# Token mixer of a two-layer trunk: projections reordered, stick queries and keys made with stationary weights, small attention steps regrouped, masks moved to VectorE

## The chip, the cores and the metric

The kernel runs on one core of a Trainium2 chip. The metric is the device time of one execution in microseconds (us). The engines are named as the profile names them: PE is TensorE (PEld its weight loads), DVE is VectorE, ACT is ScalarE, POOL is GpSimd, and SP issues most DMAs.

## The reference, cut to what matters

```python
h = x
for i in range(DEPTH):                                  # DEPTH 2, SEQ 256, D_MODEL 1024
    f = swiglu(rms_norm(h, ffn1_pre_g[i]), ffn1_w_gu[i], ffn1_w_down[i])     # D_FF 2816
    h = h + 0.5 * rms_norm(f, ffn1_post_g[i])
    u = rms_norm(h, mix_pre_g[i])
    sb_q, sb_k, sb_v, df_q, df_k, df_v, g_sb, g_df = jnp.split(u @ w_in[i], split_at, axis=-1)
    ...
    # stick breaking, 8 heads of 64:  z = q k^T / 8, strict causal mask
    log_one_minus = jnp.where(strict, jax.nn.log_sigmoid(-z), 0.0)
    later = lax.cumsum(log_one_minus, axis=3, reverse=True) - log_one_minus
    w = jnp.where(strict, jnp.exp(jax.nn.log_sigmoid(z) + later), 0.0)       # o_sb = w @ v
    ...
    # differential, 4 heads, two components of 64 each, rotary on df_q and df_k
    z = jnp.where(causal, z, -jnp.inf)
    probs = jax.nn.softmax(z, axis=-1)
    a = probs[:, :, 0] - lam * probs[:, :, 1]                                # o_df = rms_norm(a @ v)
    ...
    merged = jax.nn.sigmoid(g_sb) * y_sb + jax.nn.sigmoid(g_df) * y_df       # y = o @ w_branch
    h = h + rms_norm(merged @ w_out[i], mix_post_g[i])
    # then a second feed-forward part like the first, and a gated per-layer embedding
```

`w_in` has ten blocks of 512 columns: stick q, k, v, differential q, k, v, and four blocks of gates.

## The kernel before

All products are made in "exact" arithmetic: a float32 operand is split into a high part (fp32r) and a low part, and a product is hi\*hi + hi\*lo + lo\*hi. Weights come in units of 128x2048 float32, which are 512 rows by 512 columns of a `w_in` block. SP loads a unit into one of three slots; ACT makes its high part `w_hi` (`high`, L646, scaled by the norm's gain); DVE makes its low part `w_lo` (`low`, L1084, four instructions of 128x512); PE then uses it. A slot comes free when PE is through with the unit that stood in it.

The order of all work is written by hand, as one stream for each engine, with semaphores between them. The mixer of a layer is a loop over `m`. For m = 0 to 19 PE multiplies the two units of block j = m // 2 (half = m % 2) into two PSUM banks, one for each half `t` of the 256 tokens; m = 20 and 21 are the stick branch's output product. In iteration m ACT and DVE prepare unit m + 2, and do their part of the attention steps that stand at that place. On PE small steps stand either between the two token halves of unit m (`middle`) or behind it (`behind`).

A wide unit (`wide`, L1473 to L1475) has the activations stationary and 512 weight columns moving: 24 matmuls of 512 columns, result tokens x columns. The feed-forward loop also has a flat unit (`flat_gate_up`, L1591 and L1601): 128x128 blocks of the weights are stationary and the tokens move, 16 matmuls of 512 columns (high and low tokens side by side) and 16 of 256, result columns x tokens.

The stick and differential q and k come out as tokens x columns; ACT copies each to `slab` with the row scale (`keep`), POOL applies the rotary to the two differential ones (`rope`, four instructions for each of the two token halves), and PE transposes each (`turn_four`, 8 transposes, L1692) into `sbq_t`, `sbk_t`, `dfq_t`, `dfk_t`. `v_sb` and `v_df` are scaled into place by DVE (L1314).

The four stick pairs go through `stick_scores` (PE), three ACT and four DVE steps (`stick_soft`), `stick_later` (PE), exponential (ACT), `cap` (DVE), `stick_values` (PE). The four differential heads go through `masked` and `diff_scores` (PE), maximum (DVE), exponential (ACT), mixing (DVE), `diff_turn` (PE), copy (ACT), `diff_values` (PE) and a norm (ACT, POOL, DVE). The tables at L54 to L59 say at which half iteration each stands: stick pair n has its scores at m = 6 + 3n, differential head n at m = 12 + 2n. `kept(i, j, t)` makes PE wait until half t of block j has left PSUM. In the profile and in the rows below, `ps` is the PSUM.

## Time and profile before

| | |
|---|---|
| median of 3 runs | 1187.6 us (1187.34 to 1187.7) |
| the profiled execution | 1187.24 us, of it 1185.2 us from the first to the last instruction |
| busy | PE 1173.8 us (99%), DVE 848.7 us (72%), ACT 719.9 us (61%), POOL 92.9 us (8%) |
| TensorE's granted clock | 0.999 of full speed |
| mixer, layer 0 | m = 3 to 19 run from 218.66 us to 337.06 us |

In the timeline a matmul's busy time reaches past the start of the next one, since they are pipelined; what a matmul costs in a stream is the distance between two starts. The same holds, by a few hundredths of a microsecond, for DVE and ACT.

### The profile page before, as it was taken

The page shows a single profiled execution, that of the slowest core. Times are in us where ns is not written, and L with a number is a line of the kernel's source. Part 1 is how long each engine was busy: PE and PEld are TensorE (multiplying, and loading weights), DVE is VectorE, ACT ScalarE, POOL GpSimd, SP SyncE. Part 2 cuts the span into 40 slices and gives each one's busy share as a digit, 9 for nine tenths or more (in the row PEclk, how much of TensorE's full clock was granted, in tenths as well). Part 3 has the DMA queues.
Part 4 walks back from the last instruction along what each step waited for, and adds up shares of the span by engine and source line. Part 5 has one row for each costly group of instructions (what it writes and reads, how often), then busy time and mean ns, then how long its engine had stood idle before and what let it go on. Part 6 is the DMA issues. An engine that isn't in the chain of part 4 may idle for free.

```text
span 1185.2 us, 17137 instructions
## 1 busy us (share of the span) xinstructions
PE 1173.8 (99%) x6013; PEld 984.4 (83%) x6013; DVE 848.7 (72%) x1235; ACT 719.9 (61%) x1163; POOL 92.9 (8%) x157
## 2 busy tenths in 40 slices
PE   8999999999999999999999999999999999999997
PEld 7888888888788888888888888888877888888886
DVE  5766777588667866676787776676976776767666
ACT  6655556666665755564685655576656666555555
POOL 4000000042000100000110000010600010000002
PEclk9999999999999999999999999999999999999999
DMA  8656565553345555556546565756343456556550
GB/s 269 232 183 201 171 218 192 198 178 118 132 178 178 178 196 194 191 172 230 178 158 203 175 209 178 249 162 208 114 159 133 169 178 213 175 179 206 183 196 36
DMA packets 138654, 215.36 MB, mean 182 GB/s; under 512 B 6958, under 2 KB 97904, under 8 KB 138608
## 3 DMA queue, kind: packets, MB, share of 16 engines
q1 hardware_dynamic: 135808, 208.43, 52.9%
q10 hardware_dynamic: 2576, 6.29, 1.6%
q8 instruction: 28, 0.46, 0.2%
q14 instruction: 18, 0.15, 0.0%
q0 software_dynamic: 224, 0.04, 0.0%
HBM read 213.68 MB, written 1.05 MB: 181 GB/s over the span
## 4 chain that ended last, share of the span: by engine, by line
PE 96%; ACT 2%; DVE 1%; DMA 1%; issue 0%; POOL 0%; SPq 0%; DVEq 0%; POOLq 0%; ACTq 0%
PE ps L1591 22%; PE ps L1473 19%; PE ps L1475 19%; PE ps L1474 19%; PE ps L1601 12%; PE ps L1520 2%; PE ps L1692 1%; DMA raw<-in_w_ple_proj 1%; PE ps L1723 1%; DVE w_lo L1084 0%; ACT w_hi L646 0%; PE ps L1736 0%; PE ps L1709 0%; ACT prob L804 0%; PE ps L1752 0%
## 5 line engine op out<-in xcount | busy, mean ns | idle before, releaser
L1084 DVE SCALAR_TENSOR_TENSOR w_lo<-raw,g_layer,w_hi 128x512 fp32r<-128x512 f32 (+1 forms) x504 | 369.6, 793 | 131.4 <-ACT w_hi L646 131.4
L646 ACT ACTIVATE w_hi<-raw,g_layer 128x512 fp32r<-128x512 f32 (+1 forms) x524 | 346.9, 732 | 113.5 <-PE ps L1601 97.0
L1591 PE MATMUL ps<-x_both,w_hi 128*128 128x512 f32 x1152 | 287.7, 392 | 0.0
L1473 PE MATMUL ps<-w_hi,x_both 128*128 128x512 f32 x640 | 257.4, 402 | 0.0
L1475 PE MATMUL ps<-w_hi,x_both 128*128 128x512 f32 x640 | 250.2, 391 | 0.0
L1474 PE MATMUL ps<-w_lo,x_both 128*128 128x512 f32 x640 | 249.6, 390 | 0.0
L1591 PEld LDWEIGHTS ps<-x_both,w_hi 128*128 128x128 f32 x1152 | 209.4, 189 | 39.3 <-issue 0.3
L1081 DVE TENSOR_TENSOR w_lo<-raw,w_hi 128x1024 fp32r<-128x1024 f32 x114 | 134.7, 1221 | 55.0 <-ACT w_hi L643 55.0
L643 ACT ACTIVATE w_hi<-raw 128x1024 fp32r<-128x1024 f32 x114 | 114.7, 1052 | 91.7 <-PE ps L1475 91.6
L1601 PEld LDWEIGHTS ps<-x_both,w_lo 128*128 128x128 f32 x1152 | 152.6, 191 | 8.4
L1601 PE MATMUL ps<-x_both,w_lo 128*128 128x256 f32 x1152 | 156.0, 283 | 0.0
L1473 PEld LDWEIGHTS ps<-w_hi,x_both 128*128 128x128 f32 x640 | 120.2, 188 | 27.1 <-issue 3.3
L1475 PEld LDWEIGHTS ps<-w_hi,x_both 128*128 128x128 f32 x640 | 120.1, 188 | 26.1
L1474 PEld LDWEIGHTS ps<-w_lo,x_both 128*128 128x128 f32 x640 | 120.4, 188 | 22.8
L1473 PE MATMUL ps<-w_hi,ht_hi 128*128 128x512 f32 x320 | 124.9, 390 | 0.0
L1475 PE MATMUL ps<-w_hi,ht_lo 128*128 128x512 f32 x320 | 124.6, 389 | 0.0
L1474 PE MATMUL ps<-w_lo,ht_hi 128*128 128x512 f32 x320 | 124.5, 389 | 0.0
L728 ACT ACTIVATE glu<-glu 128x512 f32<-128x512 f32 x36 | 22.8, 633 | 78.5 <-DVE glu L1130 78.5
L1475 PEld LDWEIGHTS ps<-w_hi,ht_lo 128*128 128x128 f32 x320 | 60.1, 188 | 12.5
L1474 PEld LDWEIGHTS ps<-w_lo,ht_hi 128*128 128x128 f32 x320 | 60.1, 188 | 12.4
L1473 PEld LDWEIGHTS ps<-w_hi,ht_hi 128*128 128x128 f32 x320 | 60.1, 188 | 12.3
L536 POOL TENSOR_TENSOR ms_post<-mean_post,eps_half 128x1 f32<-128x1 f32 x8 | 2.4, 305 | 548.6 <-ACT tmp L694 548.6
(217 smaller groups left out, 1008.7 us busy)
## 6 DMA issues: line engine op xcount, KB each, us to landing
raw<-in_ffn_w_gu SPq DMA_DIRECT2D x170, 512.0 KB, 4.6
...
```

Of the source, the lines that this page charges most:

```text
L643: last = act.activation(w_hi[:, s, part], raw[:, s, part], ACT.Copy)
L646: last = act.activation(w_hi[:, s, part], raw[:, s, part], ACT.Copy, scale=g_layer[:, g:g + 1])
L728: act.activation(glu_g, glu_g, ACT.Silu).then_inc(silu_done, 2)
L1081: last = dve.tensor_tensor(w_lo[:, s, part], raw[:, s, part], whi[:, part], ALU.subtract)
L1084: last = dve.scalar_tensor_tensor(out=w_lo[:, s, part], in0=raw[:, s, part], scalar=g_layer[:, g:g + 1], in1=whi[:, part], op0=ALU.mult, o ...
L1473: pe.matmul(dst, x_h, w_h, start=first, stop=False, **group)
L1474: pe.matmul(dst, x_h, w_l, start=False, stop=False, **group)
L1475: return pe.matmul(dst, x_l, w_h, start=False, stop=last, **group)
L1520: mm = pe.transpose(x_bank(i, q, idx)[:, k * P:(k + 1) * P], src[:, (4 * n + k) * P:(4 * n + k + 1) * P], ident[:, :])
L1591: mm = pe.matmul(dst, w_hi[:, s, cols], x_both[:, :, 4 * half + k, :], start=half == 0 and k == 0, stop=stop and k == 3, skip_group_check= ...
L1601: mm = pe.matmul(bank(FLAT_BANK[j])[:, 0:SEQ], w_lo[:, s, cols], x_hi[:, 4 * half + k, :], start=False, stop=False, skip_group_check=True)
L1692: mm = pe.transpose(dst[:, k * SEQ + t * P:k * SEQ + (t + 1) * P], src[:, t, k * P:(k + 1) * P], ident[:, :])
```

## The change

- Blocks of `w_in` are taken in another order: differential q, differential k, stick q, stick k, differential v, stick v, gates (`W_IN_BLOCK`). Block j still has m = 2j and 2j + 1.
- Stick q and k (m = 4 to 7) are made as flat units (`flat_win`). Their results stand as columns x tokens, so their two `turn_four` go. Instead ACT copies the part made of low tokens to `flat_copy` (`keep_flat`), and DVE adds the other part and multiplies by the row scale (`add_flat`, four instructions for a block). The row scale is needed along the free axis, so it is spread by DVE (`spread_r`), transposed by PE (`turn_r`, two transposes) and copied by ACT (`keep_r`) at m = 1 and 2.
- POOL's rotary for differential q stands behind block 0 instead of block 3, that of k behind block 1 instead of block 4. The transposes stand behind m = 4 and 6 instead of 9 and 11.
- Stick pair n and differential head n share their places: scores of both behind m = 7 + 3n; `stick_later` and `diff_turn` in the middle of m = 9 + 3n, `diff_values` behind it. `stick_values` stand in the middle of 12, behind 13 and 16, and in the middle of 19, and write to a bank of their own (3 or 5).
- The causal mask of the differential scores was two bf16 matmuls of 256 columns (`masked`); now it is two minimum instructions on DVE in PSUM (`cap_df`), 128x256 each, for each head.

```diff
-SBQ, SBK, SBV, DFQ, DFK, DFV = range(6)
+DFQ, DFK, SBQ, SBK, DFV, SBV = range(6)
+W_IN_BLOCK = (3, 4, 0, 1, 5, 2, 6, 7, 8, 9)
 
 PAIRS = SB_HEADS // 2
-SB_SCORE = {12 + 6 * n: n for n in range(PAIRS)}
-SB_LATER = {15 + 6 * n: n for n in range(PAIRS)}
-SB_VALUE = {17 + 6 * n: n for n in range(PAIRS)}
-DF_Z0, DF_T0, DF_P0 = 12, 13, 14
-BY_ACT = (0, 1, 3, 4, 6, 7, 8, 9)
-QK_ORDER = {SBQ: 0, SBK: 1, DFQ: 2, DFK: 3}
+SB_SCORE = {15 + 6 * n: n for n in range(PAIRS)}
+SB_LATER = {18 + 6 * n: n for n in range(PAIRS)}
+SB_VALUE = {slot_: n for n, slot_ in enumerate((24, 27, 33, 38))}
+DF_SCORE = {7 + 3 * n: n for n in range(DF_HEADS)}
+DF_TURN = {9 + 3 * n: n for n in range(DF_HEADS)}
+BY_ACT = (DFQ, DFK, 6, 7, 8, 9)
...
+        df_slabs = [[x[:, t, 0:W] for t in range(TT)] for x in (tmp, gates[:, 0, :, :])]
+        flat_copy = w_att[:, :, 0:SEQ]
...
+        SB_FLAT = {SBQ: (0, 4), SBK: (0, 2)}
+        VALUE_BANK = (3, 3, 3, 5)
+
+        def outs(n):
+            return bank(VALUE_BANK[n])[:, 0:SEQ].rearrange("p (t q) -> p t q", t=TT)
...
+            def keep_flat(i, m, j):
+
+                for x, b in enumerate(SB_FLAT[j]):
+                    n = 4 * i + 2 * (j - SBQ) + x
+                    wait_product(act, win_done, 10 * i + j + 1, i, U_WIN + m, x)
+                    act.wait_ge(flat_added, n)
+                    act.activation(flat_copy, flat_pair(b)[1], ACT.Copy, scale=SB_D ** -0.5 if j == SBQ else 1.0
+                                   ).then_inc(flat_kept, 1)
 
...
+            def add_flat(i, j):
+
+                for x, b in enumerate(SB_FLAT[j]):
+                    n = 4 * i + 2 * (j - SBQ) + x + 1
+                    dst = (sbq_t, sbk_t)[j - SBQ][:, 2 * x:2 * x + 2, :]
+                    dve.wait_ge(flat_kept, n)
+                    dve.scalar_tensor_tensor(out=dst, in0=flat_pair(b)[0], scalar=SB_D ** -0.5 if j == SBQ else 1.0,
+                                             in1=flat_copy, op0=ALU.mult, op1=ALU.add).then_inc(flat_added, 1)
+                    dve.wait_ge(flat_added, n)
+                    dve.wait_ge(r_kept, nth_r(i, 1))
+                    dve.tensor_tensor(dst, dst, r_cols.to_broadcast([P, 2, SEQ]), ALU.mult).then_inc(sb_ready, 1)
+
...
                     if m == 1:
+                        dve.wait_ge(pre_scale, 8 * i + 4)
+                        spread_r(i)
...
-                    if m in (5, 11):
+                    if m in (5, 7):
+                        add_flat(i, m // 2)
+                    if m in (9, 11):
                         j = m // 2
                         for t in range(TT):
                             wait_product(dve, win_done, 10 * i + j + 1, i, U_WIN + m, t)
                             dve.tensor_scalar((v_sb, v_df)[j == DFV][:, t, :], bank(WIN_BANK[j % 2][t]),
...
+                        for c in range(2):
+                            last = dve.tensor_tensor(diagonal(DF_BANK[c]), diagonal(DF_BANK[c]),
+                                                     cap_df[:, :, :].to_broadcast([P, 2, P]), ALU.min)
+                        last.then_inc(d_capped, 1)
+                        dve.wait_ge(d_capped, DF_HEADS * i + hd + 1)
...
-                pe.wait_ge(sb_turned, 2 * i + 2)
+                pe.wait_ge(sb_ready, 4 * i + 3 + n // 2)
                 if n:
-                    pe.wait_ge(os_split, PAIRS * i + n)
+                    pe.wait_ge(s_weight, PAIRS * i + n)
...
-                pe.wait_ge(kept_dve, 4 * i + 2)
+                kept(i, (SBV, SBV, 7, 8)[n], 1)
+                if n:
+                    pe.wait_ge(os_split, PAIRS * i + n)
...
-                for c in range(2):
-                    masked(DF_BANK[c], mask_df)
                 for c, rows in enumerate(HEAD_ROWS):
-                    pe.matmul(bank(DF_BANK[c])[:, 0:P], dfq_t[rows, hd, 0:P], dfk_t[rows, hd, 0:P], start=False,
+                    pe.matmul(bank(DF_BANK[c])[:, 0:P], dfq_t[rows, hd, 0:P], dfk_t[rows, hd, 0:P], start=True,
                               stop=False, skip_group_check=True)
                 for c, rows in enumerate(HEAD_ROWS):
...
                 pe.wait_ge(d_kept, DF_HEADS * i + hd + 1)
-                pe.wait_ge(kept_dve, 4 * i + 4)
+                kept(i, DFV, 0)
                 dst, c = bank(DF_BANK[1]), slice(hd * DF_V, (hd + 1) * DF_V)
                 pe.matmul(dst[:, 0:P], mixed_t[:, 0:P], v_df[:, 0, c], start=True, stop=True, skip_group_check=True)
                 pe.matmul(dst[:, P:SEQ], mixed_t[:, P:SEQ], v_df[:, 0, c], start=True, stop=False,
                           skip_group_check=True)
+                kept(i, DFV, 1)
...
                 stick(i, 2 * m)
-                if 0 <= m - DF_P0 < 2 * DF_HEADS and (m - DF_P0) % 2 == 0:
-                    diff_values(i, (m - DF_P0) // 2)
+                if m in DF_TURN:
+                    diff_turn(i, DF_TURN[m])
...
-                    turn_four(pair(QK_PAIR), slab).then_inc(qk_turned, 1)
+                    turn_r(i, 1, QK_PAIR)
                 if m == 4:
-                    pe.wait_ge(kept_act, 16 * i + 4)
-                    pe.wait_ge(sb_turned, 2 * i + 1)
-                    turn_four(pair(QK_PAIR), slab).then_inc(qk_turned, 1)
-                if m == 9:
+                    pe.wait_ge(r_kept, nth_r(i, 1))
                     pe.wait_ge(roped, 4 * i + 2)
-                    pe.wait_ge(sb_turned, 2 * i + 2)
-                    turn_four(pair(QK_PAIR), slab).then_inc(qk_turned, 1)
-                if m == 11:
+                    turn_four(pair(QK_PAIR), df_slabs[0]).then_inc(qk_turned, 1)
+                if m == 6:
                     pe.wait_ge(roped, 4 * i + 4)
                     pe.wait_ge(df_turned, 2 * i + 1)
-                    turn_four(pair(QK_PAIR), slab).then_inc(qk_turned, 1)
+                    turn_four(pair(QK_PAIR), df_slabs[1]).then_inc(qk_turned, 1)
                 stick(i, 2 * m + 1)
-                if 0 <= m - DF_Z0 < 2 * DF_HEADS and (m - DF_Z0) % 2 == 0:
-                    diff_scores(i, (m - DF_Z0) // 2)
-                if 0 <= m - DF_T0 < 2 * DF_HEADS and (m - DF_T0) % 2 == 0:
-                    diff_turn(i, (m - DF_T0) // 2)
+                if m in DF_SCORE:
+                    diff_scores(i, DF_SCORE[m])
+                if m in DF_TURN:
+                    diff_values(i, DF_TURN[m])
...
+            def bank_free(i, j, t):
+
+                if j in (DFV, SBV):
+                    pe.wait_ge(flat_added, 4 * i + 2 * (j - DFV) + 2)
+                elif j > SBV:
+                    kept(i, j - 2, t)
+                    if t == 1 and j in (7, 9):
+                        pe.wait_ge(os_split, PAIRS * i + {7: 2, 9: 3}[j])
...
+            def flat_win(i, m, j, half, x):
+
+                s, b = slot(U_WIN + m), SB_FLAT[j][x]
+                if half == 0:
+                    if x:
+                        kept(i, j - 2, 1)
+                    elif j == SBK:
+                        pe.wait_ge(flat_added, 4 * i + 1)
+
+                def long(stop):
+
+                    for n in range(2):
+                        dst = bank(b + n).rearrange("p (a n) -> p a n", a=2)
+                        for k in range(4):
+                            cols = slice(k * W + (2 * x + n) * P, k * W + (2 * x + n + 1) * P)
+                            mm = pe.matmul(dst, w_hi[:, s, cols], x_both[:, :, 4 * half + k, :],
+                                           start=half == 0 and k == 0, stop=stop and k == 3, skip_group_check=True)
+                    return mm
...
+                    return mm
+
...
+                short()
+                mm = long(True)
+                if x == 0:
+                    mm.then_inc(win_done, 1)
+                return mm
 
             def mixer(i):
                 def first_win(s, t, before):
...
+                        if j in SB_FLAT:
+                            mm = flat_win(i, m, j, half, t)
+                            if t == 0:
+                                middle(i, m)
+                            continue
+                        if half == 0:
+                            bank_free(i, j, t)
...
```

DVE around the iterations 4 to 6: behind the small `neg_lam` steps stood the low part of unit 7 and the scaling of `v_sb`.

```order
L1304 TENSOR_TENSOR neg_lam<-lam_e 128x1 [waits lam_exp]
L1307 TENSOR_TENSOR neg_lam<-neg_lam,neg_init 128x1 [waits lam_step]
L1084 SCALAR_TENSOR_TENSOR w_lo<-raw,g_layer,w_hi 128x512 [waits hi_ready]
L1084 SCALAR_TENSOR_TENSOR w_lo<-raw,g_layer,w_hi 128x512
L1084 SCALAR_TENSOR_TENSOR w_lo<-raw,g_layer,w_hi 128x512 [waits hi_ready]
L1084 SCALAR_TENSOR_TENSOR w_lo<-raw,g_layer,w_hi 128x512
L1314 TENSOR_SCALAR v_sb<-ps,r_pre 128x512 [waits win_done]
L1314 TENSOR_SCALAR v_sb<-ps,r_pre 128x512 [waits units_used]
```

Now the copy of `dfq_t` stands ahead of that low part (L1100), and `add_flat` for stick q behind it.

```order
L1338 TENSOR_TENSOR neg_lam<-lam_e 128x1 [waits lam_exp]
L1341 TENSOR_TENSOR neg_lam<-neg_lam,neg_init 128x1 [waits lam_step]
L1369 COPY dfq_t<-ps 128x1024 [waits qk_turned]
L1100 SCALAR_TENSOR_TENSOR w_lo<-raw,g_layer,w_hi 128x512 [waits hi_ready]
L1100 SCALAR_TENSOR_TENSOR w_lo<-raw,g_layer,w_hi 128x512
L1100 SCALAR_TENSOR_TENSOR w_lo<-raw,g_layer,w_hi 128x512 [waits hi_ready]
L1100 SCALAR_TENSOR_TENSOR w_lo<-raw,g_layer,w_hi 128x512
L1301 SCALAR_TENSOR_TENSOR sbq_t<-ps,w_att 128x512 [waits flat_kept]
L1305 TENSOR_TENSOR sbq_t<-sbq_t,prob 128x512 [waits r_kept,flat_added]
L1301 SCALAR_TENSOR_TENSOR sbq_t<-ps,w_att 128x512 [waits flat_kept]
```

The first of these `add_flat` instructions is behind one more long copy and the whole low part; PE's m = 6 waits for it (`flat_added`).

PE where scores begin: a differential head's scores stood by themselves behind m = 12, ahead of the next unit.

```order
L1698 MATMUL ps<-mask_df,ident_b 128x2x128 [waits df_turned]
L1698 MATMUL ps<-mask_df,ident_b 128x2x128
L1749 MATMUL ps<-dfk_t,dfq_t 128x128 x2
L1752 MATMUL ps<-dfk_t,dfq_t 128x256 x2
L1473 MATMUL ps<-w_hi,x_both 128x512 [waits split_done]
L1474 MATMUL ps<-w_lo,x_both 128x512
```

Now the first stick pair and the first head stand together behind m = 7, whose last flat matmuls are the first row here.

```order
L1877 MATMUL ps<-x_both,w_hi 128x512 x8
L1746 MATMUL ps<-sbq_t,sbk_t 128x256 [waits sb_ready]
L1746 MATMUL ps<-sbq_t,sbk_t 128x256
L1749 MATMUL ps<-sbq_t,sbk_t 128x128 x2
L1786 MATMUL ps<-dfk_t,dfq_t 128x128 [waits df_turned]
L1786 MATMUL ps<-dfk_t,dfq_t 128x128
L1789 MATMUL ps<-dfk_t,dfq_t 128x256 x2
L1512 MATMUL ps<-w_hi,x_both 128x512 [waits flat_added,split_done]
```

The two masks are gone, and the scores of both kinds stand without a unit between them; m = 8 begins in the last row.

PE at the first stick values: before, they stood behind m = 8, three units after `v_sb`'s own (m = 5).

```order
L1474 MATMUL ps<-w_lo,x_both 128x512
L1475 MATMUL ps<-w_hi,x_both 128x512
L1736 MATMUL ps<-w_att,v_sb 64x128 [waits kept_dve,s_capped]
L1736 MATMUL ps<-w_att,v_sb 64x128 x5
L1473 MATMUL ps<-w_hi,x_both 128x512 [waits split_done]
L1474 MATMUL ps<-w_lo,x_both 128x512
```

Now they stand in the middle of m = 12, half a unit after `v_sb`'s own (m = 11), with `stick_later` (the last two rows here) and then `diff_turn` behind them.

```order
L1513 MATMUL ps<-w_lo,x_both 128x512
L1514 MATMUL ps<-w_hi,x_both 128x512
L1775 MATMUL ps<-w_att,v_sb 64x128 [waits kept_dve,s_capped]
L1775 MATMUL ps<-w_att,v_sb 64x128 x5
L1760 MATMUL ps<-sp_hi,neg_tri 128x384 [waits s_soft]
L1761 MATMUL ps<-sp_hi,neg_one 128x128
```

The wait for `kept_dve` is for both halves of `v_sb`. In the same way the first `diff_values` now stand right behind m = 9, the unit that makes `v_df`.

## Rows read from the trace of the kernel before

**Rows 1.** The page: busy us of each engine, TensorE's clock, the chain by engine
```profile
PE 1173.8 (99%) x6013; PEld 984.4 (83%) x6013; DVE 848.7 (72%) x1235; ACT 719.9 (61%) x1163; POOL 92.9 (8%) x157
...
PEclk9999999999999999999999999999999999999999
...
PE 96%; ACT 2%; DVE 1%; DMA 1%; issue 0%; POOL 0%; SPq 0%; DVEq 0%; POOLq 0%; ACTq 0%
```

**Rows 2.** The chain in order of time (start us, us, what), feed-forward loop
```profile
45.33 1.81 PE ps L1591 x8
...
61.92 1.81 PE ps L1591 x8
```

**Rows 3.** Timeline of PE in the mixer, layer 0 (start us, us, engine, line, op, out<-in, count [idle])
```profile
218.66 1.03 PE L1692 MATMUL ps<-ident,tmp 128*128 128x128 f32 x8
219.45 0.48 PE L1473 MATMUL ps<-w_hi,x_both 128*128 128x512 f32 x1
219.77 0.40 PE L1474 MATMUL ps<-w_lo,x_both 128*128 128x512 f32 x1
...
230.24 0.39 PE L1475 MATMUL ps<-w_hi,x_both 128*128 128x512 f32 x1
```

**Rows 4.** Timeline of PE: stick scores, stick values, differential scores, each standing alone
```profile
239.29 0.39 PE L1475 MATMUL ps<-w_hi,x_both 128*128 128x512 f32 x1
...
240.80 0.40 PE L1474 MATMUL ps<-w_lo,x_both 128*128 128x512 f32 x1
...
255.17 0.39 PE L1475 MATMUL ps<-w_hi,x_both 128*128 128x512 f32 x1
...
256.63 0.39 PE L1474 MATMUL ps<-w_lo,x_both 128*128 128x512 f32 x1
...
284.39 0.39 PE L1698 MATMUL ps<-mask_df,ident_b 128*128 128x256 bf16 x2
284.71 0.49 PE L1749 MATMUL ps<-dfk_t,dfq_t 64*128 64x128 f32 x4
...
285.90 0.39 PE L1474 MATMUL ps<-w_lo,x_both 128*128 128x512 f32 x1
```

**Rows 5.** Timeline of PE: longest idle in the mixer, longest of all after the start
```profile
310.40 0.39 PE L1475 MATMUL ps<-w_hi,x_both 128*128 128x512 f32 x1
311.01 0.49 PE L1767 MATMUL ps<-v_df,mixed_t 128*128 128x128 f32 x2 [0.21 <-ACT mixed_t L813]
...
9.63 0.50 PE L1473 MATMUL ps<-w_hi,p_hi 128*128 128x512 f32 x1 [1.02 <-DVE w_lo L1062]
```

**Rows 6.** Timeline of DVE: low parts before, during and after the rotary
```profile
212.93 2.74 DVE L1084 SCALAR_TENSOR_TENSOR w_lo<-raw,g_layer,w_hi 128x512 fp32r<-128x512 f32 x4 [2.94 <-ACT w_hi L646]
...
246.44 4.78 DVE L1084 SCALAR_TENSOR_TENSOR w_lo<-raw,g_layer,w_hi 128x512 fp32r<-128x512 f32 x4
...
267.08 1.21 DVE L1329 COPY dfq_t<-ps 128x1024 f32<-128x1024 f32 x1
268.21 5.32 DVE L1084 SCALAR_TENSOR_TENSOR w_lo<-raw,g_layer,w_hi 128x512 fp32r<-128x512 f32 x4
```

**Rows 7.** Timeline of POOL (rotary) and of ACT (the first kept product)
```profile
247.09 1.30 POOL L577 TENSOR_TENSOR tmp<-tmp,rope_c 128x512 f32<-128x512 f32 x1 [35.67 <-ACT tmp L842]
...
252.51 1.30 POOL L577 TENSOR_TENSOR tmp<-tmp,rope_c 128x512 f32<-128x512 f32 x1
...
214.03 1.24 ACT L842 ACTIVATE tmp<-ps,r_query 128x512 f32<-128x512 f32 x2
```

**Rows 8.** Timeline of DVE: one differential and one stick step, value projection
```profile
285.68 1.02 DVE L1323 TENSOR_REDUCE neg_max<-ps 128x2 f32<-128x256 f32 x2 [1.76 <-PE ps L1752]
...
287.60 0.76 DVE L1255 TENSOR_TENSOR soft<-soft,cap_sb 128x256 f32<-128x256 f32 x2
...
290.98 0.75 DVE L1084 SCALAR_TENSOR_TENSOR w_lo<-raw,g_layer,w_hi 128x512 fp32r<-128x512 f32 x1
...
278.42 1.39 DVE L1314 TENSOR_SCALAR v_df<-ps,r_pre 128x512 f32<-128x512 f32 x2
```

More of the change, by code:

```diff
@@ L242, in trunk_kernel @@
         d_score = sem("d_score")
+        d_capped = sem("d_capped")
         d_max = sem("d_max")
@@ new lines, in diff_keep, with diff_square @@
+            def diff_keep(i, hd):
+                act.wait_ge(d_turned, DF_HEADS * i + hd + 1)
+                act.activation(mixed_t[:, :], bank(DF_BANK[0])[:, 0:384], ACT.Copy).then_inc(d_kept, 1)
+            def diff_square(i, hd):
+                act.wait_ge(d_value, DF_HEADS * i + hd + 1)
+                if hd:
+                    act.wait_ge(d_square, DF_HEADS * i + hd)
+                for t in range(TT):
+                    last = act.activation(squares[:, t * P:(t + 1) * P], bank(DF_BANK[1])[:, t * P:(t + 1) * P],
+                                          ACT.Square, scale=DF_V ** -0.5, accum_out=mean_sub[:, t:t + 1])
+                last.then_inc(d_square, 1)
@@ L1285, in mixer @@
                     elif 2 * m in SB_VALUE:
-                        low(i, U_WIN + m + 2, 8 + 4 * (m % 2), halves=(0,))
+                        gain = 8 + 4 * (m % 2) if m < 18 else None
+                        low(i, U_WIN + m + 2, gain, halves=(0,))
                         stick_out(i, 2 * m)
-                        low(i, U_WIN + m + 2, 8 + 4 * (m % 2), halves=(1,))
+                        low(i, U_WIN + m + 2, gain, halves=(1,))
                     elif m < 18:
@@ L1735, in stick_values @@
                         c = (2 * n + e) * SB_D
-                        mm = pe.matmul(bank(SB_BANK[t])[rows, OUT_COLS], v_sb[:, keys, c:c + SB_D],
+                        mm = pe.matmul(outs(n)[rows, t, :], v_sb[:, keys, c:c + SB_D],
                                        w_att[:, e, cols], start=first, stop=last, skip_group_check=True)
@@ new lines, in flat_win, with short @@
+            def flat_win(i, m, j, half, x):
[13 more added lines that the diff above has]
+                    return mm
+                def short():
+                    for n in range(2):
+                        for k in range(4):
+                            cols = slice(k * W + (2 * x + n) * P, k * W + (2 * x + n + 1) * P)
+                            mm = pe.matmul(bank(b + n)[:, 0:SEQ], w_lo[:, s, cols], x_hi[:, 4 * half + k, :],
+                                           start=False, stop=False, skip_group_check=True)
+                    return mm
+                if half == 0:
+                    long(False)
+                    return short()
+                short()
[3 more added lines that the diff above has]
+                return mm
```

181 lines of the change are left out of this document (81 added, 100 removed).

## Prediction, made before the changed kernel was run

> **What bounds the kernel now.** I read the page first: PE is busy 1173.8 of 1185.2 us, 96% of the chain that ended last is PE, and its clock stays at full speed (2.4 GHz) in all 40 slices [rows 1]. So the time is the sum of PE's starts plus its few waits. I then took PE's timeline for prices, as distances between starts, since busy times overlap; and DVE's, POOL's and ACT's timelines to see what else could come to stand in PE's way.
>
> In the mixer the two wide units from 219.45 to the start at 230.24 and 0.23 more take 11.02 us for 48 matmuls, 0.09 of it a slow start [rows 3]: 5.46 us a unit, 0.2275 a matmul. One turn of the feed-forward loop is 16.59 us [rows 2]; less a 24-matmul unit of 5.46 that leaves 5.57 for each of its two flat units. Between the starts at 310.40 and 311.01, 0.61 instead of 0.23, PE waited longest inside the mixer [rows 5]. Everything else there is PE's own work, so a change must take work from PE, and must not make it wait.
>
> **PE's work, for one layer.** (1) The `turn_four` of stick q and k go. One costs 219.77 - 218.66 - 0.23 = 0.88 us, eight transposes at 0.11 [rows 3]: -1.76. `turn_r` comes, two transposes: +0.22.
>
> (2) Stick scores alone cost 240.80 - 239.29 less two matmuls = 1.05. Differential scores alone cost 285.90 - 284.39 - 0.23 = 1.28, of which the masks 0.32 [rows 4]. A group of 64-row matmuls pays on entering and leaving: the matmul ahead of the stick scores and the one behind take some 0.1 more each, and so do the first and last inside. Joined and without masks I count 1.05 + 1.28 - 0.32 - 0.3 = 1.71 (between 1.5 and 2.0, if two or no such payments go). Four times -0.62 is -2.5.
>
> (3) Stick values alone cost 256.63 - 255.17 - 0.455 = 1.0 [rows 4]. Two of the four now stand ahead of scores and share their entry: -0.3 each, -0.6 (0 if a 64-column and a 64-row group share nothing). Later and turn steps are joined four times instead of twice: -0.1. Fewer restarts: -0.2.
>
> (4) Four wide units become flat: 4 x (5.57 - 5.46) = +0.45.
>
> (5) The wait of 0.4 goes with the place it stood at.
>
> Sum: -1.76 + 0.22 - 2.5 - 0.6 - 0.1 - 0.2 + 0.45 - 0.4 = -4.9 a layer, -9.8 us for two (bounds -7.5 and -11). The minimum instructions on DVE replace PE work; DMAs stay, only the block's address changes; POOL loses its bf16 set-up, in the first microseconds, where nobody waits for it.
>
> **New waits, for one layer.** All three come from DVE, which works in strict order and now has more ahead of what PE wants.
>
> *A, at m = 6.* This flat unit writes banks 0 and 1, which the first half of stick q (m = 5) filled; they are free once `add_flat` has read them. PE: m = 2 ends at 218.66 as now; 0.22, 5.46, 5.57, 0.88 and 5.57 take it to 236.4.
>
> DVE: its low part from 212.93 takes 2.74 us for four instructions, 0.665 each [rows 6]. POOL's rotary now follows the product ACT keeps at 214.03 (first half 0.68 later, then 0.14 to POOL) [rows 7], so at 214.85. One token half took 5.4 us (247.09 to 252.51) [rows 7], and there are four. So POOL works until 236.5, where before this stretch was free of it. Under it DVE's four take 4.78 us, the first of them ahead of POOL's start at 247.09, so (4.78 - 0.67) / 3 = 1.37 each; and 5.32, 1.33 each [rows 6, 7]. I take 1.37. From 212.93: three at the free pace, one slow, then the row spread and the lambda sums (an estimate, 1.0) to 217.4; the low parts of units 4, 5 and 6, 12 x 1.37 = 16.4, to 233.8; lambda again and the copy of `dfq_t`, 1.21 under POOL's work [rows 6] and 0.3, to 235.3; unit 7's low part, nearly one instruction slow and three free, 3.3, to 238.6; `add_flat`, as one low instruction with its end 0.75, to 239.3; 0.1 for PE to start. PE waits from 236.4 to 239.4: 3.0 us. At 1.25 each it is 2.2, at 1.5 it is 4.0. If the rotary did not slow DVE at all it is 0: 13 instructions fewer at 1.37, 9 us, are more than the 3.0.
>
> Why DVE is slowed: the Trainium skill, SBUF - State Buffer, section "SBUF: two separate sides", says that GpSimd and a VectorE instruction with two SBUF inputs take one port pair in turn, each for its whole instruction. By that rule 16 POOL instructions let 16 such DVE instructions through in 21.6 us, 1.35 each, which makes A 2.9 us where my rows make it 3.0. It speaks against moving the rotary to where DVE is needed within half a unit.
>
> *B, behind m = 9.* `diff_values` need `v_df`, m = 9's own product. The joint scores behind m = 7 end (call it 0). DVE is held by `add_flat` of stick k for 0.8; then two minima 0.78 (as two `cap` on SBUF, 0.76 [rows 8]; not seen on PSUM, 0.7 to 1.1), the diff and stick step 5.30 (285.68 to 290.98) [rows 8], two low parts 5.3, `cap` 0.73, `v_df` first half 0.7: 13.7. PE: 0.1 + 5.46 + 2.73 + 1.43 (later and turn) + 2.73 = 12.45. It waits 1.4, and some 0.2 more for the second half: 1.6 (1.0 to 2.2).
>
> *C, in the middle of m = 12.* `stick_values` need both halves of `v_sb`, m = 11's product. From the end of the scores behind m = 10: DVE 0.1 + 0.78 + 5.30 + 2.65 (low part) + 1.39 (`v_sb`, as the two of `v_df` [rows 8]) = 10.2, and 0.1 to start PE: 10.3. PE is there after 0.1 + 5.46 + 2.73 = 8.3. Wait 2.0 (1.7 to 2.5). For the later pairs values and gates are kept early, and I find no wait: `diff_turn` has 1.0 us or more to spare each time.
>
> Waits: 3.0 + 1.6 + 2.0 = 6.6 a layer. Each starts from a point where DVE waited for PE, so they add up.
>
> **Sum.** 2 x (6.6 - 4.9) = +3.4 on the profiled 1187.24, so 1190.6; that execution is 0.36 below the median, which gives 1191.0.
>
> **Rivals.** *Free rotary.* A is small, because POOL's instructions run faster when DVE yields, or DVE gets in more often than in rows 6. For it: rows 6 are two samples, taken while DVE did other things in between. Against: both are at 1.33 or more. With A at 0.5: 2 x (4.1 - 4.9) = -1.6, 1186.0. The total turns from slower to faster once A is under 1.3 us.
>
> *All hidden.* None of the waits is there, because DVE has more room than I count: -9.8, 1177.8. Against it: B and C are sums of rows seen in this very order of work, and only 1 to 2 us of error is in each.
>
> *DVE stays behind.* A wait at m = 6 also delays stick k's `add_flat`, so the first scores behind m = 7 wait as well (I count DVE ready 0.1 us before PE), and later turns miss their 1.0 us: 1 to 2 us more a layer, 1191.5 to 1196.
>
> *The clock falls.* PE's longest pause now between matmuls after the start is 1.02 us, with full clock behind it [rows 5, 1]; A would be three times that, and what the clock then does no row shows. If it fell to 1.2 GHz for some 3 us behind each A, it would cost 1.5 us each: +3, 1194. The Trainium skill, TensorE: Matmul & The Clock Gate, section "Why this matters for your kernels", advises against idle gaps of about this length in the middle of a kernel; by it this rival would be live.
>
> *The regrouping saves less on PE* (no shared entries, bf16 masks cheaper than 0.32): -7.5 instead of -9.8, 1193.
>
> **How the numbers follow.** Forecast with three waits, 1188.5 to 1193.5: 0.48. DVE stays behind or the clock falls: 0.14. Less saved on PE: 0.05. Free rotary, 1184.5 to 1188: 0.22. All hidden: 0.11. The range 1184.0 to 1194.5 leaves out all hidden and the far end of the slow rivals. A measurement of this kernel can tell 0.2% (2.4 us) from no change. Above 1190.0: two thirds of the forecast's share and all but little of the slow ones, 0.51; within: 0.26, from the forecast's lower part and half of free rotary; below 1185.2: 0.23. The likeliest case's own range is 1188.5 to 1193.5.
>
> **What the profile after would show.** PE idle of about 3 us ahead of the first matmul of the third flat unit, released by DVE's `sbq_t`; about 1.5 ahead of the first `diff_values`, by `v_df`; about 2 ahead of the first `stick_values`, by `v_sb`; none of these three and the rest is wrong with them. Low parts of 1.2 to 1.8 us each on DVE between 215 and 236 us. The joint scores 1.7 us from start to start, 0.88 for each of two `turn_four` less, flat units at 5.57. The clock at full speed throughout, or this is where the forecast errs. It is wrong above all if DVE keeps pace with the rotary, or if PE's small groups cost other than the sum of their rows.

## The result, and the profile after

The changed kernel takes 1201.7 us (median; 1201.3 to 1202.4) against 1187.5 us before (1187.3 to 1187.7): ratio 1.0121, 95% interval 1.0107 to 1.0135. It is slower by 14.2 us. The profiled execution spans 1199.6 us, where that of before spanned 1185.2. Of all executions of the kernels below, four took 1452 to 6678 us; the ratios leave these slow runs out, the medians hold them and move by at most 0.3 us for it.

The page of the changed kernel: busy us of each engine, PE's busy share and TensorE's clock in 40 slices, and the chain that ended last by engine.
```profile
PE 1172.9 (98%) x6033; PEld 989.5 (82%) x6033; DVE 867.2 (72%) x1269; ACT 717.2 (60%) x1161; POOL 92.9 (8%) x154
...
PE   8999999899999999999999999998999999999997
...
PEclk9999999999999999999999999999999999999999
...
PE 89%; DVE 8%; ACT 1%; issue 1%; DMA 1%; SPq 0%; DVEq 0%; POOLq 0%; POOL 0%; ACTq 0%
```
Against [rows 1], DVE's share of the chain went from 1% to 8%. That names the engine to look at, not the size of the loss: 7% of the span would be 84 us. The rest of the page shows little: two of PE's slices read 8 instead of 9, PE's busy time is nearly unchanged (1172.9 against 1173.8 us), because matmuls that run slowly count as busy, and a clock that falls for a few us did not change the digit of any 30 us slice. So I went on to what PE waits for (us in total, times, longest), and to PE's timeline.
```profile
PE ps L1877 <- DVE sbq_t L1301: 9.4, 2, 4.7
PE ps L1775 <- DVE v_sb L1350: 4.4, 2, 2.2
PE ps L1804 <- DVE v_df L1350: 1.7, 2, 0.9
```
```profile
234.72 2.00 PE L1877 MATMUL ps<-x_both,w_hi 128*128 128x512 f32 x8
241.43 3.75 PE L1877 MATMUL ps<-x_both,w_hi 128*128 128x512 f32 x8 [4.71 <-DVE sbq_t L1301]
244.98 0.41 PE L1886 MATMUL ps<-x_both,w_lo 128*128 128x256 f32 x1
...
255.56 0.70 PE L1746 MATMUL ps<-sbq_t,sbk_t 64*128 64x256 f32 x4
...
257.07 0.50 PE L1512 MATMUL ps<-w_hi,x_both 128*128 128x512 f32 x1
...
269.33 0.39 PE L1514 MATMUL ps<-w_hi,x_both 128*128 128x512 f32 x1
270.59 0.46 PE L1804 MATMUL ps<-v_df,mixed_t 128*128 128x128 f32 x2 [0.87 <-DVE v_df L1350]
...
286.63 0.39 PE L1514 MATMUL ps<-w_hi,x_both 128*128 128x512 f32 x1
289.19 0.88 PE L1775 MATMUL ps<-w_att,v_sb 128*64 128x128 f32 x12 [2.18 <-DVE v_sb L1350]
290.00 0.69 PE L1760 MATMUL ps<-sp_hi,neg_tri 128*128 128x384 f32 x1
290.49 0.31 PE L1761 MATMUL ps<-sp_hi,neg_one 128*128 128x128 f32 x1
```
The three forecast waits are there, at the forecast places, in both layers. As a distance between starts less one matmul, the first is 4.87 us in layer 0 and 4.89 in layer 1 (A); the others are 1.03 (B, and 0.2 for the second half of `v_df`) and 2.34 (C). Two rows show something else. The eight flat matmuls from 241.43 take 3.75 us, where the eight from 234.72 took 2.00. The 128x384 matmul at 290.00 holds the engine for 0.49 us until the next start; the same four at m = 9 take 0.17 to 0.23 (265.37 to 266.40), and run 9 below shows 0.28 at this very place. The same trace by stretches (us, busy us of PE, PEld, DVE, ACT and POOL with instructions, granted clock, DMA share, GB/s) says why:
```profile
230.00:236.00 6.00, 6.00 (x41) 5.45 (x40) 6.00 (x5) 3.16 (x5) 5.78 (x5) 1.00 0.54 175
236.00:241.00 5.00, 0.72 (x4) 0.26 (x2) 4.97 (x8) 0.00 (x0) 0.69 (x1) 0.78 0.66 210
241.00:243.00 2.00, 1.57 (x4) 1.31 (x5) 1.93 (x4) 1.62 (x3) 0.00 (x0) 0.50 0.52 96
243.00:246.00 3.00, 3.00 (x13) 2.52 (x12) 3.00 (x5) 1.42 (x3) 0.00 (x0) 0.57 0.77 290
246.00:250.00 4.00, 4.00 (x30) 3.67 (x29) 0.07 (x1) 0.74 (x2) 0.00 (x0) 1.00 0.69 215
286.00:289.00 3.00, 1.01 (x5) 0.51 (x3) 3.00 (x6) 1.40 (x3) 0.00 (x0) 1.00 0.13 14
289.00:291.00 2.00, 1.80 (x15) 1.66 (x16) 1.85 (x5) 0.38 (x1) 0.00 (x0) 0.74 0.80 266
291.00:294.00 3.00, 3.00 (x13) 2.79 (x13) 2.00 (x4) 1.19 (x2) 0.00 (x0) 0.60 0.59 180
```
The granted clock, full before the wait, is 0.50 behind A and at 0.6 to 0.7 on average behind C: it fell to 1.2 GHz and came back. I size that by distances between starts: from A's end to the `turn_four` of k 7.57 us, where kernels with a full clock there show 5.69; from the first stick values to the next `diff_values` 6.67 us against 5.10. So the clock costs 1.9 us behind A (1.4 in layer 1) and 1.6 behind each C.

DVE's timeline shows why A is 4.9 and not 3.0:
```profile
213.10 3.78 DVE L1100 SCALAR_TENSOR_TENSOR w_lo<-raw,g_layer,w_hi 128x512 fp32r<-128x512 f32 x4 [2.98 <-ACT w_hi L656]
216.81 0.83 DVE L1136 COPY mixed_t<-r_pre 128x256 f32<-128x256 f32 x1
217.56 0.82 DVE L1332 TENSOR_TENSOR lam_pr<-lam_layer 128x128 f32<-128x128 f32 x1
...
218.62 16.92 DVE L1100 SCALAR_TENSOR_TENSOR w_lo<-raw,g_layer,w_hi 128x512 fp32r<-128x512 f32 x12
235.46 1.25 DVE L1338 TENSOR_TENSOR neg_lam<-lam_e 128x1 f32<-128x1 f32 x1
...
236.81 1.22 DVE L1369 COPY dfq_t<-ps 128x1024 f32<-128x1024 f32 x1
237.95 2.73 DVE L1100 SCALAR_TENSOR_TENSOR w_lo<-raw,g_layer,w_hi 128x512 fp32r<-128x512 f32 x4
240.60 0.68 DVE L1301 SCALAR_TENSOR_TENSOR sbq_t<-ps,w_att 128x512 f32<-128x512 f32 x1
```
The twelve large instructions take (235.46 - 218.62) / 12 = 1.40 us each, forecast 1.37. What I had not priced is the small ones under the rotary: a copy of 128x256 takes 0.83 us, a product of 128x128 0.82, and a difference of 128x1 1.25. In the run without the rotary they take 0.41, 0.28 and 0.15.

### The profile page after: what moved, and what is told of

It is laid out like the page before. It is cut to its first block, busy times and chain, and to the rows that moved or that the text cites. A ratio compares the mean times of both kernels' runs of the same rounds, so it can differ in the third digit from the quotient of the medians.

```text
span 1199.6 us, 17214 instructions
## 1 busy us (share of the span) xinstructions
PE 1172.9 (98%) x6033; PEld 989.5 (82%) x6033; DVE 867.2 (72%) x1269; ACT 717.2 (60%) x1161; POOL 92.9 (8%) x154
## 4 chain that ended last, share of the span: by engine, by line
PE 89%; DVE 8%; ACT 1%; issue 1%; DMA 1%; SPq 0%; DVEq 0%; POOLq 0%; POOL 0%; ACTq 0%
PE ps L1633 22%; PE ps L1512 16%; PE ps L1514 16%; PE ps L1513 16%; PE ps L1643 11%; DVE w_lo L1100 5%; PE ps L1559 2%; PE ps L1877 2%; PE ps L1886 1%; DMA raw<-in_w_ple_proj 1%; PE ps L1760 1%; PE ps L1775 1%; PE ps L1746 0%; DVE soft L1257 0%; PE ps L1734 0%
## 5 line engine op out<-in xcount | busy, mean ns | idle before, releaser
L1100 DVE SCALAR_TENSOR_TENSOR w_lo<-raw,g_layer,w_hi 128x512 fp32r<-128x512 f32 (+1 forms) x504 | 375.7, 807 | 134.5 <-ACT w_hi L656 134.5
L1512 PE MATMUL ps<-w_hi,x_both 128*128 128x512 f32 x576 | 231.2, 401 | 0.0
L1514 PE MATMUL ps<-w_hi,x_both 128*128 128x512 f32 x576 | 225.1, 391 | 0.0
L1513 PE MATMUL ps<-w_lo,x_both 128*128 128x512 f32 x576 | 224.7, 390 | 0.0
L1512 PEld LDWEIGHTS ps<-w_hi,x_both 128*128 128x128 f32 x576 | 108.4, 188 | 23.7 <-issue 3.0
L1514 PEld LDWEIGHTS ps<-w_hi,x_both 128*128 128x128 f32 x576 | 108.1, 188 | 23.5
L1513 PEld LDWEIGHTS ps<-w_lo,x_both 128*128 128x128 f32 x576 | 108.5, 188 | 20.7
```

The lines of the kernel that those rows point to most:

```text
L1100: last = dve.scalar_tensor_tensor(out=w_lo[:, s, part], in0=raw[:, s, part], scalar=g_layer[:, g:g + 1], in1=whi[:, part], op0=ALU.mult, o ...
L1512: pe.matmul(dst, x_h, w_h, start=first, stop=False, **group)
L1513: pe.matmul(dst, x_h, w_l, start=False, stop=False, **group)
L1514: return pe.matmul(dst, x_l, w_h, start=False, stop=last, **group)
```

## Experiments

All twelve change only a few lines. Times are medians; the kernel before gave 1187.3 to 1187.5 beside them. The account behind them adds up, for each run, what its own trace shows: waits and slow stretches read as above, against the changed kernel's.

**1. No rotary.** POOL rotates one head of eight only (the output is changed by that).
```diff
-                    pool.tensor_tensor(slab_c[:, t, :] ..., x, rope_c ..., ALU.mult)
-                    pool.tensor_tensor(y[:, :, 0:32], ..., ALU.mult)
-                    pool.tensor_tensor(y[:, :, 32:64], ..., ALU.mult).then_inc(rope_parts, 1)
+                    pool.tensor_tensor(slab_c[:, t, 0:64], xs[:, 0:64], rope_c[:, t, :], ALU.mult).then_inc(rope_parts, 1)
                     pool.wait_ge(rope_parts, 4 * i + 2 * k + t + 1)
-                    pool.tensor_tensor(xs, slab_c[:, t, :], rope_b[:, t, :], ALU.add).then_inc(roped, 1)
+                    pool.tensor_tensor(xs[:, 0:64], slab_c[:, t, 0:64], rope_s[:, t, :], ALU.add).then_inc(roped, 1)
```


> The changed kernel with POOL's rotary cut to one head of eight: per token half two instructions of 128x64 instead of four on 128x512 (the output is changed by that). Theory (POOL's rotary holds DVE back until stick k's first half must wait for add_flat, and the clock then falls): the wait of 4.9 us inside m = 6 and the half-rate matmuls behind it (2.0 us) are gone in both layers, the waits behind m = 9 and in the middle of m = 12 stay: 1201.7 - 13.8 = 1188. Rival (DVE is late by its own order of work, POOL counts for little): a wait of 2 us or more stays at m = 6, 1195 or more.

Measured 1186.5, ratio 0.9988 (0.9978 to 0.9998). What PE waits for now begins with these lines; the one at m = 6 is gone:
```profile
PE ps L1767 <- DVE v_sb L1342: 4.4, 2, 2.2
PE ps L1796 <- DVE v_df L1342: 1.7, 2, 0.9
```
Without the rotary DVE even waits for ACT ahead of two low parts in that stretch. With DVE's order as it is, A needs the rotary; B and C stand without it. It is 1.5 us better than expected, and in the profiled execution the clock did not fall behind C in layer 1, which is 1.6.

**2. v_df and v_sb by ACT.**
```diff
+                    elif j in (SBV, DFV):     # ACT's keep
+                        act.activation((v_sb, v_df)[j == DFV][:, t, :], src, ACT.Copy,
+                                       scale=r_pre[:, t:t + 1]).then_inc(kept_dve, 1)
-                    if m in (9, 11):          # DVE
-                        ... dve.tensor_scalar((v_sb, v_df)[j == DFV][:, t, :], ...)
```


> The changed kernel with v_df and v_sb (units 9 and 11) scaled and kept by ACT instead of DVE. Theory (DVE's own order makes the waits B and C; the clock falls behind C): the 2.3 us in the middle of m = 12, the 2.0 us of half-rate matmuls behind it and nearly all of the 1.25 us behind m = 9 go: 1201.7 - 11 = 1191. The wait at m = 6 stays 4.9. Rival (something else that DVE does at m = 11 is as late, as stick's cap): C shrinks by the two v_sb instructions alone, 1.4 us a layer, and the clock still falls: 1198.

Measured 1193.3, ratio 1.0053 (1.0036 to 1.0070). C is gone with the half-rate stretch behind it, and of B 0.6 remains:
```profile
PE ps L1874 <- DVE sbq_t L1304: 9.4, 2, 4.7
...
PE ps L1805 <- ACT v_df L859: 0.7, 2, 0.3
```
It is 2 us short of the forecast: 1.2 for that rest of B, and behind the unchanged A the clock stayed low longer (2.8 and 2.3 us lost instead of 1.9 and 1.4).

**3. Useless transposes inside the waits.**
```diff
+                        kept(i, DFK, 1)       # m = 6, ahead of the wait for add_flat
+                        for n in range(38):
+                            pe.transpose(bank(2)[:, n % 4 * P:(n % 4 + 1) * P], ident[:, :], ident[:, :])
                         pe.wait_ge(flat_added, 4 * i + 1)
...
+                        if m == 12 and t == 0:
+                            kept(i, DFV, 1)
+                            for n in range(18):
+                                pe.transpose(bank(5)[:, n % 4 * P:(n % 4 + 1) * P], ident[:, :], ident[:, :])
```


> The changed kernel, and PE makes 38 useless transposes of the identity (0.11 us each, 4.2 us) into a free bank just ahead of the wait for add_flat at m = 6 and 18 (2.0 us) ahead of the wait for v_sb in the middle of m = 12. They lie inside the waits, which go on as long as before. Theory (the matmuls behind both waits run at half rate because PE paused and its clock fell): the granted clock stays at full level there, 2.0 us come back four times: 1201.7 - 8 = 1193.7. Rival (they are slow for another reason, such as weights or inputs that come late): 1201.7 or a little more.

Measured 1194.9, ratio 1.0064 (1.0047 to 1.0081). PE's timeline, and the stretches behind the wait:
```profile
236.48 4.31 PE L1871 MATMUL ps<-ident 128*128 128x128 f32 x38
241.25 2.11 PE L1880 MATMUL ps<-x_both,w_hi 128*128 128x512 f32 x8 [0.47 <-DVE sbq_t L1301]
```
```profile
236.00:241.00 5.00, 4.79 (x41) 4.40 (x39) 4.97 (x8) 0.00 (x0) 0.60 (x1) 1.00 0.68 211
241.00:243.00 2.00, 1.75 (x8) 1.45 (x9) 1.93 (x4) 1.71 (x3) 0.00 (x0) 1.00 0.55 131
```
The wait ends where it did, the clock stays at 1.00, and eight flat matmuls take 2.11 us instead of 3.75. More work on PE makes the kernel 6.8 us faster. The clock's part is shown, and its size by rows is 1.9 + 1.4 + 2 x 1.6 = 6.5 us.

**4. All three waits at once.** Edit 2; ACT copies `dfq_t` and `dfk_t`; the first half of stick q's `add_flat` ahead of unit 7's low part; the lambda difference at m = 6.

> The changed kernel with the three new waits attacked at once: ACT instead of DVE copies dfq_t and dfk_t out of PSUM and keeps v_df and v_sb, DVE makes the first half of stick q's add_flat ahead of its low part for m = 7, and the difference of the lambdas moves from m = 4 to m = 6. Theory (all of the loss is these waits and the clock behind them, and PE's own work is 4.9 us a layer less than before the change, as forecast): 1187.5 - 9.8 = 1177.7, or from the changed kernel 1201.7 - 25 = 1177. Rival (the saving on PE is smaller than forecast, and part of what I take for new waits was always there): 1181 to 1186. Rival (ACT becomes late in its turn): above 1186 with waits for ACT at the next high part.

Measured 1180.3, ratio 0.9941 (0.9925 to 0.9958): 7.2 us faster than before the change. Two small waits are left, 0.6 behind m = 9 and a new one of 0.9 ahead of the first scores:
```profile
249.28 0.70 PE L1747 MATMUL ps<-sbq_t,sbk_t 64*128 64x256 f32 x4 [0.85 <-DVE sbk_t L1315]
```
ACT's copy of `dfk_t` stands ahead of its next high part, which begins at 243.80 us (241.92 in run 5, without that copy); DVE's low part waits 1.34 us for it, and stick k's `add_flat` stands behind that.

**5. dfk_t back on DVE.** As 4, only `dfq_t` copied by ACT.

> As all_moved, but DVE copies dfk_t again as in the changed kernel (ACT copies dfq_t alone). In all_moved ACT made its high part for m = 9 some 1.1 us later because of that copy, DVE's low part and stick k's add_flat came behind it, and the first joint scores waited 0.9 us a layer for sbk_t. Theory (that wait is ACT's lateness): it goes, 1180.3 - 1.8 = 1178.5, and the wait at m = 6 stays away. Rival (DVE's copy of 1.2 us holds add_flat as much): 1180.3 or more.

Measured 1180.1, ratio 0.9939 (0.9925 to 0.9953). A miss: the wait shrank from 0.9 to 0.6 us only, because DVE's own copy takes most of what ACT's lateness had cost. DVE's timeline has 0.15 + 0.16 us of lambda work and the copy (1.22) ahead of the low part, and `add_flat` starts at 247.36, against 247.81 in run 4.

**6. As 5, masks of the differential scores back on PE.**
```diff
+                for c in range(2):
+                    pe.matmul(diagonal(DF_BANK[c]), ident_b[:, :], mask_df ..., start=True, stop=False, ...)
-                        for c in range(2):
-                            last = dve.tensor_tensor(diagonal(DF_BANK[c]), diagonal(DF_BANK[c]), cap_df ..., ALU.min)
```


> As k_on_dve, with the masks of the differential scores back on PE as before the change (two bf16 matmuls of 256 columns ahead of each head's scores, no minimum on DVE). It has no large waits, so it prices the masks on PE alone. Forecast's term: 0.32 us a head for the masks, 2.6 us for eight heads; and they stand between the 64-row matmuls of both kinds, which ends the joint group, 0.3 more a head. So 1178.5 + 2.6 to 5.0 = 1181.1 to 1183.5. Rival (DVE's time without the minimum gives some back): 1179.

Measured 1184.8, ratio 0.9979 (0.9969 to 0.9988), so 4.7 us more. The joint scores take 2.03 us instead of 1.51 from their first start to the next unit's, 4.2 us for eight: 0.32 for the masks and 0.2 for the matmuls on either side of them.

**7. The same masks back on PE in the changed kernel.**

> The changed kernel with the masks of the differential scores back on PE: one part of the change undone. PE does 0.32 to 0.62 us more a head (1.3 to 2.5 a layer); DVE's chain to v_df and to v_sb is 0.78 shorter, so the waits behind m = 9 and in the middle of m = 12 shrink by 0.78 each, 1.56 a layer. Theory A (a pause of 1.55 us still makes the clock fall): 1201.7 + 2 x (1.9 - 1.56) = 1202.4. Theory B (it does not, as the 1.26 us behind m = 9 doesn't): 4 us less, 1198.4.

Measured 1200.4, ratio 1.0110 (1.0095 to 1.0126), between both theories. C is 1.78 and its clock stays up, as theory B has it; but it and B shrink by 0.6 each, not 0.78, and behind A the clock cost 1.3 and 2.8. In stretches across C:
```profile
286.00:289.00 3.00, 1.38 (x13) 0.91 (x13) 3.00 (x6) 0.88 (x2) 0.00 (x0) 1.00 0.25 31
289.00:291.00 2.00, 2.00 (x20) 1.83 (x17) 1.84 (x5) 0.61 (x2) 0.00 (x0) 1.00 1.00 381
```
So the masks' move, +4.2 us of PE work when undone, is worth next to nothing where it stands (undone, the kernel is 1.3 us faster): it lengthens DVE's chain ahead of the two waits and C by enough for the clock to fall.

**8. add_flat first.**
```diff
+                    if m == 5:
+                        add_flat(i, SBQ, (0,))
                     ... low(i, U_WIN + m + 2, ...)
                     if m in (5, 7):
-                        add_flat(i, m // 2)
+                        add_flat(i, m // 2, (1,) if m == 5 else (0, 1))
```


> The changed kernel, but DVE makes the first half of stick q's add_flat ahead of its low part for m = 7 instead of behind it. That low part took 2.65 us of the wait at m = 6: it falls from 4.87 to 2.2. Theory (the low part is the last link, and a pause of 2.2 us makes the clock fall as the 2.34 us in the middle of m = 12 does): 1201.7 - 5.3 = 1196.4, half-rate matmuls still behind the wait. Rival (the clock stays up behind the shorter pause): 1192.4. Rival (something else holds the wait): 1201.

Measured 1192.8, ratio 1.0048 (1.0032 to 1.0063). A is 2.2 us as expected, and the rival is right on the clock: 1.00 behind A, while behind C, 2.34 as before, it falls. Stretches behind A, and behind C:
```profile
239.00:242.00 3.00, 3.00 (x18) 2.63 (x17) 3.00 (x6) 2.44 (x4) 0.00 (x0) 1.00 0.23 81
...
286.00:289.00 3.00, 3.00 (x13) 2.71 (x12) 2.15 (x5) 1.19 (x2) 0.00 (x0) 0.51 0.58 190
```

**9. Lambda difference at m = 6 only.**

> The changed kernel with only the difference of the lambdas moved from m = 4 to m = 6, past the end of POOL's rotary. It is 128 x 1 and takes 0.15 us when POOL is idle, 1.25 us under the rotary. Theory (that instruction, both inputs in SBUF, was held until POOL's ended, and its 1.25 us were part of the wait): the wait at m = 6 falls from 4.87 to 3.6, 1201.7 - 2.5 = 1199.2, and at m = 6 it costs 0.15. Rival (another instruction is held in its place: POOL and DVE take turns, and whichever is next waits): 4.7 or more stays, 1201.5.

Measured 1198.1, ratio 1.0091 (1.0076 to 1.0106). A falls by 1.41 us, one for one with the 1.25 and 0.16 of that work. And in layer 0 the clock stays up behind a C of the same length as in the changed kernel:
```profile
288.52 0.88 PE L1775 MATMUL ps<-w_att,v_sb 128*64 128x128 f32 x12 [2.18 <-DVE v_sb L1350]
289.32 0.44 PE L1760 MATMUL ps<-sp_hi,neg_tri 128*128 128x384 f32 x1
289.60 0.22 PE L1761 MATMUL ps<-sp_hi,neg_one 128*128 128x128 f32 x1
```

**10. Lambda difference at m = 6, and dfq_t copied by ACT.**

> The changed kernel, with ACT instead of DVE copying dfq_t out of PSUM (1.22 us) and the difference of the lambdas made at m = 6 instead of m = 4 (1.25 us under POOL's rotary). DVE's order is else as it was. Theory (all that stands ahead of add_flat on DVE adds to the wait at m = 6 one for one): 4.87 - 2.5 = 2.4. If the clock falls behind it: 1201.7 - 5 = 1196.7; if not, as behind the 2.2 us of add_early: 1192.7.

Measured 1197.7, ratio 1.0079 (1.0064 to 1.0094). My theory fell, with 2.4 us expected for A: taking 1.2 us more off DVE than run 9 leaves A at 3.40 instead of 3.46. Two low instructions of that stretch on DVE:
```profile
234.62 2.92 DVE L1104 SCALAR_TENSOR_TENSOR w_lo<-raw,g_layer,w_hi 128x512 fp32r<-128x512 f32 x2
```
With the copy gone, unit 7's first low instruction starts at 235.77, still under POOL's last rotary instruction, and takes 1.77 us instead of 0.74. The copy out of PSUM took 1.21 to 1.22 with and without POOL at work; it had stood where POOL did not hurt, and its place was taken by an instruction that POOL holds.

**11. Half the useless transposes.** 19 and 5 instead of 38 and 18.

> As warm, with half the useless transposes: 19 (2.1 us) at the start of the wait at m = 6, so that PE stands still for the 2.7 us behind them, and 5 (0.55 us) ahead of the wait for v_sb, with 1.8 us of standstill behind them. Theory (only the last standstill counts for the clock, 1.8 us keep it, 2.7 us do not): full cost behind m = 6, none behind the middle of m = 12: 1201.7 - 2 x 1.6 = 1198.5. Rival (the work of the last microseconds counts together): in between, half the gain of warm at both places.

Measured 1197.6, ratio 1.0081 (1.0067 to 1.0096). A standstill of 2.8 us at A lowered the clock in layer 0 (1.5 us lost) and not in layer 1; the 1.9 us at C did not. PE's timeline of layer 1 at A, six matmuls in 1.65 us, at full rate:
```profile
827.92 2.24 PE L1871 MATMUL ps<-ident 128*128 128x128 f32 x19
832.67 1.65 PE L1880 MATMUL ps<-x_both,w_hi 128*128 128x512 f32 x6 [2.51 <-DVE sbq_t L1301]
```
The stretches behind A in layer 0 and in layer 1 (restarts at 243.05 and 832.67), granted clock 0.50 and 1.00:
```profile
244.00:247.00 3.00, 3.00 (x12) 2.52 (x11) 2.97 (x5) 2.13 (x4) 0.00 (x0) 0.50 0.92 331
832.00:835.00 3.00, 2.33 (x12) 1.98 (x13) 2.93 (x6) 2.29 (x4) 0.00 (x0) 1.00 0.58 147
```
So neither expectation is met: C behaves as the theory has it, A goes both ways. The profiled execution (1198.0) lost 1.7 us before the mixer; what the others (1195.3 to 1199.3) lost and where is not shown.

**12. The repaired version.** As 5, the lambda difference behind stick k's `add_flat` in m = 7, and
```diff
+                    elif m == 7:
+                        low(i, U_WIN + 9, 12, halves=(0,))
+                        add_flat(i, SBK, (0,))
+                        low(i, U_WIN + 9, 12, halves=(1,))
```


> As k_on_dve, with the two waits of 0.6 us (sbk_t ahead of the first joint scores) attacked: DVE makes its low part for m = 9 in two halves with the first half of stick k's add_flat between them, and the difference of the lambdas behind add_flat instead of at m = 6. Theory (add_flat stands behind 1.3 us of the low part and 0.5 us of small work that nobody needs yet): the wait goes, 1180.1 - 1.3 = 1178.8; 0.5 us a layer behind m = 9 stay. Rival (the second half of the low part becomes late for m = 9, or nothing moves since ACT's copy comes late): 1180 or more.

Measured 1179.1, ratio 0.9930 (0.9917 to 0.9943): 8.4 us faster than before the change, 22.6 faster than the changed kernel. The gain over run 5 alone is inside both intervals, but the wait for `sbk_t` is gone from the list:
```profile
PE ps L1977 <- POOL ident L491: 1.6, 1, 1.6
PE ps L1521 <- DVE w_lo L1085: 1.0, 1, 1.0
PE ps L1817 <- ACT v_df L859: 0.7, 2, 0.3
```

**The account.** Differences to the changed kernel, both layers, in us:

| run | sum of what its trace shows | measured |
|---|---|---|
| no rotary | A -9.8, clock behind A -3.3, clock behind one C -1.6 = -14.7 | -15.2 |
| v by ACT | B -1.3, C -4.7, clock behind C -3.2, behind A +1.8 = -7.4 | -8.4 |
| transposes | clock -6.5 | -6.8 |
| all three waits | A -9.8, B -1.3, C -4.7, clock -6.5, `sbk_t` +1.8 = -20.5 | -21.4 |
| `dfk_t` on DVE | the same, `sbk_t` +1.2 = -21.1 | -21.6 |
| the same, masks on PE | the same, work +4.2 = -16.9 | -16.9 |
| changed kernel, masks on PE | work +4.2, B and C -2.3, clock -2.3 = -0.4 | -1.3 |
| add_flat first | A -5.3, clock -3.3 = -8.6 | -8.9 |
| lambda later | A -2.8, clock -0.5 = -3.3 | -3.6 |
| lambda later, `dfq_t` by ACT | A -3.0, clock -0.3 = -3.3 | -4.1 |
| half the transposes | clock -5.0, ahead of the mixer +1.7 = -3.3 | -4.1 |
| repaired | A -9.8, B -1.3, C -4.7, clock -6.5 = -22.3 | -22.6 |

Each is within 1.1 us, and nearly all are short of what was measured; the sums are of one profiled execution, the measured times are medians. From the kernel before to the changed one: work -9.8, A 9.8, B 2.5, C 4.7, clock 6.5, together 13.7 of the 14.2 us measured.

## Why the prediction was wrong

The direction was right, and so was the sum of PE's work; the time, 1191.0, and the range up to 1194.5 were too low. The forecast sum had +13.2 of waits and -9.8 of work; the runs show 17.0 of waits, 6.5 of clock, and the same -9.8. Two steps failed: A was sized 3.8 us too low over both layers, and the clock's 6.5 us were not in the sum. Together that is 10.3 of the 10.7 us between forecast and measurement.

- **PE's work, -4.9 a layer: right.** The joint scores take 1.71 us, as counted: 257.07 - 255.56 = 1.51, and 0.09 and 0.11 more for the matmuls on either side. Run 6 prices the masks on PE at 0.52 a head in the joint group, of which 0.32 the masks themselves, as in the forecast; the other 0.2 is the shared entry that they would break. The sum is tested by the repaired version: -8.4 measured, with 1.2 us of B left, is -9.6. The single terms of values, restarts and flat units were not tried apart.
- **A, 3.0: right in kind, mis-sized, and the first step that failed.** Run 1 shows that it needs the rotary, runs 8 and 9 that the low part (2.66) and the lambda difference (1.41) ahead of `add_flat` on DVE add to it one for one; run 10 shows that this is no rule, since the copy's 1.2 us taken away gave 0.06. The term "the row spread and the lambda sums (an estimate, 1.0)" was 1.8 (216.81 to 218.62), "lambda again and the copy of `dfq_t` ... and 0.3" was 2.5 and not 1.5, the first low part 0.4 slower and the twelve others 0.4; unit 7's low part took 2.65, not 3.3. Together 2 us. The bound of 4.0 moved only the price of the large instructions, and those were right; the small ones had no range.
- **B, 1.6, and C, 2.0: right in cause**, 1.25 and 2.34; run 2 shows it for both. That their sum, forecast 3.6, came out at 3.59 is luck: B was forecast 0.35 too high and C 0.34 too low.
- **The clock, the step that failed worst.** "The clock falls" was a rival with a share of 0.14 together with another, priced at 1.5 us behind each A, so +3. That price, for which no row stood, came close: 1.9 and 1.4. But the fall was left out of the sum, and it came behind A and behind C, 6.5 us in all by the rows; run 3 gives 6.8. I had asked the question of A alone, because it was the longest wait; C is 2.3 us long and I took it for harmless. The Trainium skill, "TensorE: Matmul & The Clock Gate", section "Why this matters for your kernels", warns of gaps above about 3 us. A, 5.1 us from start to start, bears that out; C at 2.57 us from start to start lowered the clock in 8 of 10 cases here, so the measurement reaches further down than the rule.
- **"Free rotary" and "all hidden": wrong.** DVE and POOL took turns, one for one, at 1.40 us a turn.
- **"DVE stays behind": wrong for the changed kernel**, where the first scores behind m = 7 do not wait. A wait at that place, 0.9 us a layer, appears in run 4, but there A is gone: it comes from ACT's copy, not from A.
- The Trainium skill, "SBUF - State Buffer", section "SBUF: two separate sides", gives POOL and a DVE instruction with two inputs in SBUF, or a copy in a two-port mode, one port pair in turn, whole instruction for whole instruction. The trace agrees down to the smallest: 128x1 waited 1.1 us for its 0.15 us of work. POOL's 16 rotary instructions stand from 215.01 to 236.68 us, and 16 of DVE's were held in that time: 13 low parts and the three small ones. I had applied it to the large instructions only.

Open: why the same C of 2.57 us keeps the clock in two of ten cases, and 2.8 us at A in one of two.
